# Stick-breaking attention block: the turns of the attention weights of small query tiles, and the turns of v, gathered into fewer bunches on TensorE

## The reference, cut to what matters

```python
for blk in range(seq // Q_BLOCK):                      # Q_BLOCK = 128
    z = einsum('bhqd,bhkd->bhqk', qb, kb) * scale      # keys 0 .. (blk+1)*128
    log_one_minus = where(mask, log_sigmoid(-z), 0)
    suffix = cumsum(log_one_minus, reverse=True) - log_one_minus
    weights = where(mask, exp(log_sigmoid(z) + suffix), 0)
    out = einsum('bhqk,bhkd->bhqd', weights, vb)
```

## Time and profile before

| what | value |
|---|---|
| median of 3 runs | 788.62 us (788.29 to 788.79) |
| profiled execution | 789.4 us, of which the span of instructions is 787.7 us |
| PE busy / loads of weights | 777.6 us (99%) / 662.2 us (84%) |
| DVE busy | 581.3 us (74%) |
| ACT busy | 413.8 us (53%) |
| the four pairs of attention | about 54 to 332 us of the span, 71.0 us each |
| granted TensorE clock | 0.999 |

### The profile page before, as it was taken

One profiled execution on the slowest core, in us unless ns is written; L12 is line 12 of the kernel. 1 busy time (PEld: TensorE's weight loads), 2 busy tenths in 40 slices (PEclk: granted clock), 3 DMA queues, 4 the chain that ended last, 5 costly groups with the idle time before them and its releaser, 6 DMA issues.

```text
span 787.7 us, 11914 instructions
## 1 busy us (share of the span) xinstructions
PE 777.6 (99%) x4458; PEld 662.2 (84%) x4458; DVE 581.3 (74%) x835; ACT 413.8 (53%) x714; POOL 33.0 (4%) x30
## 2 busy tenths in 40 slices
PE   8999999999999999999999999999999999999997
PEld 6888888888888888899899888888888888888886
DVE  6649997988899798832656767755467777779986
ACT  7546666665667476522716554444333333365443
POOL 1560000000000000020000000000000000000000
PEclk9999999999999999999999999999999999999999
DMA  9772121202201121121021001344333333395222
GB/s 319 261 255 54 27 55 53 53 27 53 53 27 33 49 53 32 43 64 54 27 56 27 29 28 54 107 146 140 139 111 107 107 107 107 111 370 214 108 107 107
DMA packets 72484, 76.31 MB, mean 97 GB/s; under 512 B 3805, under 2 KB 57208, under 8 KB 71929
## 3 DMA queue, kind: packets, MB, share of 16 engines
q1 hardware_dynamic: 72242, 75.45, 30.2%
q10 hardware_dynamic: 198, 0.28, 0.1%
HBM read 55.79 MB, written 15.73 MB: 91 GB/s over the span
## 4 chain that ended last, share of the span: by engine, by line
PE 93%; ACT 2%; DVE 2%; issue 1%; DMA 1%; SPq 0%; DVEq 0%; ACTq 0%
PE pj L709 27%; PE pj L834 6%; PE tr L1008 6%; PE sc L957 6%; PE ob L957 6%; PE ob L782 4%; PE ob L1008 4%; PE pj L1008 4%; PE tr L792 4%; PE sc L1008 3%; PE pj L725 3%; PE pj L815 3%; PE sc L758 2%; PE sc L757 2%; PE tr L1064 1%; PE ob L1034 1%
## 5 line engine op out<-in xcount | busy, mean ns | idle before, releaser
L709 PE MATMUL pj<-h_lo,w_hi 128*128 128x512 f32 x336 | 133.2, 396 | 0.0
L709 PE MATMUL pj<-h_hi,w_lo 128*128 128x512 f32 x336 | 132.2, 393 | 0.0
L709 PE MATMUL pj<-h_hi,w_hi 128*128 128x512 f32 x336 | 132.1, 393 | 0.0
L1697 DVE TENSOR_TENSOR_SCAN surv<-surv,diag 128x128 f32<-128x128 f32 (+3 forms) x64 | 86.3, 1349 | 7.4 <-ACT surv L1188 7.1
L709 PEld LDWEIGHTS pj<-h_hi,w_hi 128*128 128x128 f32 x336 | 63.1, 188 | 12.6
L709 PEld LDWEIGHTS pj<-h_hi,w_lo 128*128 128x128 f32 x336 | 63.2, 188 | 12.4 <-issue 0.3
L709 PEld LDWEIGHTS pj<-h_lo,w_hi 128*128 128x128 f32 x336 | 63.1, 188 | 12.4 <-issue 0.2
L1234 ACT ACTIVATE wt_hi<-tr 128x512 fp32r<-128x512 f32 (+2 forms) x96 | 43.6, 490 | 36.5 <-PE tr L792 35.0
L1634 DVE TENSOR_TENSOR w_lo<-w_raw,w_hi 128x1024 fp32r<-128x1024 f32 x33 | 40.3, 1221 | 22.8 <-ACT w_hi L1130 22.6
L1732 DVE TENSOR_TENSOR wt_lo<-tr,wt_hi 128x512 fp32r<-128x512 f32 (+2 forms) x96 | 50.2, 550 | 7.1 <-ACT wt_hi L1234 6.6
L1701 DVE TENSOR_TENSOR beta<-beta,surv 128x128 f32<-128x128 f32 (+3 forms) x64 | 48.6, 759 | 6.5
(11 more groups left out here) (437 smaller groups left out, 1902.9 us busy)
## 6 DMA issues: line engine op xcount, KB each, us to landing
w_raw<-in_w_in SPq DMA_DIRECT2D x30, 512.0 KB, 3.8
y_scratch<-y_ring SPq DMA_DIRECT2D x28, 256.0 KB, 2.1
graw<-in_w_in SPq DMA_DIRECT2D x14, 512.0 KB, 5.1
y_back<-y_scratch SPq DMA_DIRECT2D x14, 512.0 KB, 5.2
x_t<-in_x SPq DMA_DIRECT2D x8, 512.0 KB, 6.7
wrow<-in_w_out SPq DMA_DIRECT2D x4, 1024.0 KB, 9.3
w_scratch<-wsum SPq DMA_DIRECT2D x4, 1024.0 KB, 5.0
wout_raw<-in_w_out SPq DMA_DIRECT2D x8, 512.0 KB, 7.4
```

The costliest lines, as they stand in the source:

```text
L709: mm = pe.matmul(pj[bank][:, :], (w_lo if p == 2 else w_hi)[:, slot, k, :], (h_lo if p == 1 else h_hi)[:, k, HALF * h:HALF * h + HALF], st ...
L1697: dve.tensor_tensor_scan(s[:, ::-1], s[:, ::-1], d[:, ::-1], 0.0, ALU.mult, ALU.add)\
```

## The change

The first unit of each head (1 block) is no longer turned at its own step but together with the second (2 blocks), in one round of three blocks. The third (3 blocks) is turned one step later than before, right in front of the fourth (4 blocks), each in a round of its own. Both rounds of v are turned at step 2, one right behind the other. The rounds of a pair go from 26 to 24. The number of transposes, of copies on ACT and of subtractions on DVE stays. So that the weights of the first and third unit survive one step longer, units 0 and 4 of each head get another place in their slot of `beta` (`beta_at`), and ACT waits for `w_ready` before it writes a slot of `surv` that it had been told by the turn of the unit to be read.

```diff
     for step in range(STEPS):
-        if step in (1, 2):
-            rounds.append(("v", step, step - 1))
-        if 1 <= step <= 16:
-            unit = step - 1
-            blocks = unit % 8 + 1
-            for b in range(0, blocks, 4):
-                rounds.append(("w", step, unit, b, min(4, blocks - b)))
+        if step == 2:
+            rounds += [("v", step, 0), ("v", step, 1)]
+        unit = step - 1
+        if not 1 <= step <= 16 or unit % 8 in (0, 2):
+            continue
+        blocks = unit % 8 + 1
+        if unit % 8 == 1:
+            rounds.append(("w", step, [(unit - 1, 0, 1), (unit, 0, 2)]))
+            continue
+        if unit % 8 == 3:
+            rounds.append(("w", step, [(unit - 1, 0, 3)]))
+        for b in range(0, blocks, 4):
+            rounds.append(("w", step, [(unit, b, min(4, blocks - b))]))
     return rounds
+
+def beta_at(unit):
+    return {0: 7 * P, 4: 3 * P}.get(unit % 8, 0)
...
-LAST_ROUND = {r[2]: n for n, r in enumerate(ROUNDS) if r[0] == "w"}
+LAST_ROUND = {piece[0]: n for n, r in enumerate(ROUNDS) if r[0] == "w" for piece in r[2]}
...
-                            pe.wait_ge(w_ready, 16 * i + unit + 1)
+                            pe.wait_ge(w_ready, 16 * i + r[2][-1][0] + 1)
                             pe.wait_ge(tr_free, RPP * i + R0 + n - 1)
-                            for b in range(nb):
-                                mm = pe.transpose(tr[n % 2][:, P * b:P * b + P],
-                                                  beta[:, unit % 2, P * (b0 + b):P * (b0 + b) + P], ident[:, :])
+                            at = 0
+                            for unit, b0, nb in r[2]:
+                                for b in range(b0, b0 + nb):
+                                    c0 = beta_at(unit) + P * b
+                                    mm = pe.transpose(tr[n % 2][:, at:at + P], beta[:, unit % 2, c0:c0 + P],
+                                                      ident[:, :])
+                                    at += P
                             mm.then_inc(tr_ready, 1)
...
                         act.wait_ge(scores_ready, 16 * i + step + 1)
+                        if step % 8 in (2, 4):
+                            act.wait_ge(w_ready, 16 * i + step - 1)
...
-                        act.activation(beta[:, step % 2, 0:keys].rearrange("p (c w) -> p c w", w=width), scores,
+                        c0 = beta_at(step)
+                        act.activation(beta[:, step % 2, c0:c0 + keys].rearrange("p (c w) -> p c w", w=width), scores,
                                        ACT.Sigmoid, scale=HD ** -0.5).then_inc(sig_done, 1)
-                    if step in (1, 2):
-                        act.wait_ge(wsum_stored[step + 1], 16)
+                    if step == 2:
+                        act.wait_ge(wsum_stored[2], 16)
+                        act.wait_ge(wsum_stored[3], 16)
```

More of the change, by code:

```diff
@@ L787, in pair @@
                         if r[0] == "w" and r[1] == step:
-                            unit, b0, nb = r[2:]
-                            pe.wait_ge(w_ready, 16 * i + unit + 1)
+                            pe.wait_ge(w_ready, 16 * i + r[2][-1][0] + 1)
                             pe.wait_ge(tr_free, RPP * i + R0 + n - 1)
-                            for b in range(nb):
-                                mm = pe.transpose(tr[n % 2][:, P * b:P * b + P],
-                                                  beta[:, unit % 2, P * (b0 + b):P * (b0 + b) + P], ident[:, :])
+                            at = 0
[5 more added lines that the diff above has]
+                                    at += P
                             mm.then_inc(tr_ready, 1)
@@ L1230, in pair @@
                         if r[0] == "w" and r[1] == step:
-                            unit, b0, nb = r[2:]
-                            g = unit % 8 // 2
                             act.wait_ge(tr_ready, RPP * i + R0 + n + 1)
-                            act.activation(wt_hi[g % 2][:, b0:b0 + nb, P * (unit % 2):P * (unit % 2) + P],
-                                           tr[n % 2][:, 0:P * nb].rearrange("p (b q) -> p b q", q=P),
-                                           ACT.Copy).then_inc(tr_act, 1)
+                            at = 0
+                            for unit, b0, nb in r[2]:
+                                g = unit % 8 // 2
+                                cp = act.activation(wt_hi[g % 2][:, b0:b0 + nb, P * (unit % 2):P * (unit % 2) + P],
+                                                    tr[n % 2][:, at:at + P * nb].rearrange("p (b q) -> p b q", q=P),
+                                                    ACT.Copy)
+                                at += P * nb
+                            cp.then_inc(tr_act, 1)
             with act.Fori(0, PAIRS - 1) as i:
@@ L1700, in pair @@
                         dve.wait_ge(sig_done, 16 * i + step + 2)
-                        dve.tensor_tensor(beta[:, step % 2, 0:keys], beta[:, step % 2, 0:keys],
+                        own = beta[:, step % 2, beta_at(step):beta_at(step) + keys]
+                        dve.tensor_tensor(own, own,
                                           surv[:, step % 2, 1:keys + 1], ALU.mult).then_inc(w_ready, 1)
-                    if step in (1, 2):
-                        dve.wait_ge(wsum_stored[step + 1], 16)
+                    if step == 2:
+                        dve.wait_ge(wsum_stored[2], 16)
+                        dve.wait_ge(wsum_stored[3], 16)
                     for n, r in enumerate(ROUNDS):
@@ L1727, in pair @@
                         if r[0] == "w" and r[1] == step:
-                            unit, b0, nb = r[2:]
-                            g = unit % 8 // 2
-                            qs = slice(P * (unit % 2), P * (unit % 2) + P)
                             dve.wait_ge(tr_act, RPP * i + R0 + n + 1)
[L1732 to L1735, removed]
+                            at = 0
+                            for unit, b0, nb in r[2]:
+                                g = unit % 8 // 2
+                                qs = slice(P * (unit % 2), P * (unit % 2) + P)
+                                sub = dve.tensor_tensor(wt_lo[g % 2][:, b0:b0 + nb, qs],
+                                                        tr[n % 2][:, at:at + P * nb].rearrange("p (b q) -> p b q", q=P),
+                                                        wt_hi[g % 2][:, b0:b0 + nb, qs].bitcast(F32), ALU.subtract)
+                                at += P * nb
+                            sub.then_inc(tr_free, 1)
                     if step >= 3 and step % 2:
```

## The result

The changed kernel takes 793.10 us (median of 5, 792.41 to 793.62) against 788.79 us for the kernel before in the same comparison: ratio 1.0053, 95% interval 1.0037 to 1.0069, so 2.9 to 5.4 us slower. One timing of the kernel before, 1110 us, lies 40% above the other four and is left out of the ratio.

What follows compares the result with a forecast made beforehand. PE was taken to bound the kernel; a new 0.92 us stall per pair, less savings at borders and unit 7, added 2.9 us to 788.6, giving 791.5 us. The range was 789.8 to 793.2, the forecast's own 790.6 to 792.4.

Steps and rivals of the forecast that it cites:

- What bounds the kernel: PE, busy 99% of the span, with next to no stall to remove; a new wait adds undiluted.
- the new wait: At step 2 the joint turn of units 0 and 1 waits for DVE's low part of the first v round.
- The size of the stall: Joint turn, step 2: PE ready at 132.69, released at 133.61, so 0.92 us a pair; allowed 0.7 to 1.1.
- the first link: ACT, step 1: without the v copy, `q_st` starts at that copy's old time, 126.93 instead of 127.56.
- The signs named for this place: Steps 1 and 2: `z_sig`, `z_silu`, `w_lo` about 0.6 us earlier; DVE's scan of unit 3 about 0.6 later.
- Borders: Twenty fewer switches between transposes and other matmuls save 0.5 us; bounds 0.01 to 0.09 each, 0.2 to 1.8 in all.
- What is given back: After the stall DVE gains 0.25 us on PE and keeps it until unit 7, removing a wait there.
- unit 7's 0.12 us: PE's wait for DVE at the turn of unit 7, expected to vanish in three of the four pairs.
- One of the signs of being wrong: In the profile after, pairs differing from each other by more than 0.12 us would speak against the forecast.
- The rivals without a stall: Low part of v in time: cheap borders, about 788.1 us, 10 in 100; or borders 0.09 each, 786.4, 4 in 100.
- the one with 1.55 us: Joint turn: DVE's chain starts at its old time, stall 1.55 us a pair, 793.9 us total; 9 in 100.
- the one in which half of it is swallowed: DVE-bound places further on absorb half the stall: about 1.5 us slower, 790.1 us; 7 in 100.

Runs made afterwards that it cites:

- e1: Kernel before with only the v rounds changed: both turned at step 2, every weight turn left in place; 794.41 us, ratio 1.0060.
- e2: Kernel before with only the weights gathered as in the change, v turned at steps 1 and 2 as before; 788.96 us, ratio 0.9991.
- e7: The changed kernel with both v rounds turned together at step 1 instead of step 2; 788.17 us, ratio 0.9998 to the kernel before.
- e3: The changed kernel with DVE's two low parts of v at step 2 moved ahead of the scan of unit 2; 788.62 us, ratio 0.9992 to before.
- e5: The changed kernel with a useless DVE copy of 256 columns ahead of the first low part of v; 794.02 us, ratio 1.0069 to before.
- e6: The changed kernel with the w_lo subtraction moved from the end of step 1 to behind step 2's low parts of v; 787.87 us, ratio 0.9994 to before.
- e4: Kernel before with 28 bunches split by a held-back projection matmul, adding 28 borders; 789.82 us, ratio 1.0003, stretch +0.19 us.

## Why the prediction was right, and where its terms were off

**What bounds the kernel, and the new wait: right.** One new wait a pair, at the joint turn, for the first low part of v, reached by reading the order of banks against DVE's order. e1, e2 and e7 place it in the v rounds at step 2; e3, e5 and e6 show the chain on DVE to be its whole cause.

**The size of the stall: 1.08 us, not 0.92.** PE's request was right: 133.42 - 0.75 = 132.67 against 132.69. The release came at 134.50 - 0.75 = 133.75 against 133.61. The stall is 1.08 - 0.92 = 0.16 longer: 0.02 from the request, and the 0.14 of the release stem from the first link: I let ACT's `q_st` start where the v copy had, 0.27 behind the start of the second sigmoid. It started 0.40 behind it, when the sigmoid had ended, and `z_sig`, `z_silu` and all behind it moved with it. The distances from `z_silu` to the low part of v came out as read (3.29 us forecast and measured). The signs named for this place came, with sizes off in the same way: `z_silu` 0.5 us earlier against the pair's start where 0.6 was expected, DVE's scan of unit 3 0.8 later where 0.6 was. A pair loses 1.11 us by unit 7, 0.03 more than the stall of 1.08. This term the forecast did not have, and it lies right behind the stall: the three transposes and the first score take 0.62 us there (134.50 to 135.12), in e3, without a stall, 0.57 (131.67 to 132.24).

**Borders: 0.5 us forecast, 0 found.** The term "0.04 for the v bunch and 0.02 for each of the other four" was wrong; my lower bound of 0.01 was near the truth (e4: 0.007 at most). The Trainium skill ("TensorE: Matmul & The Clock Gate", section "Single matmul latency") gives a lone matmul about 166 ns that don't depend on its columns; at that price the 28 borders of e4 would have cost an estimated 4.6 us. They cost 0.19. No run here has a lone matmul, so the figure itself is not put to the test; it doesn't apply, because a bunch of transposes doesn't break the stream.

**What is given back: wrong in its mechanism; that the amount came near is luck.** "It goes", of unit 7's 0.12 us, failed: the wait is in every kernel here. DVE did gain on PE (its scan of unit 3 was 1.57 us later than before, 136.21 against 134.64, where PE's score behind the joint turn was 1.84 later, 134.81 against 132.97), but the lead ended at unit 4, where DVE now had to wait for the copy that it had met just in time before (PE's score, kernel before; then the timeline of DVE, kernel before and the change):

```profile
132.97 0.48 PE L757 MATMUL sc<-k_hi,q_st 128*128 128x512 f32 x1
```

```profile
144.74 0.96 DVE L1701 TENSOR_TENSOR beta<-beta,surv 128x768 f32<-128x768 f32 x1
145.74 0.89 DVE L1732 TENSOR_TENSOR wt_lo<-tr,wt_hi 128x512 fp32r<-128x512 f32 x2
```

```profile
146.31 0.96 DVE L1723 TENSOR_TENSOR beta<-beta,surv 128x768 f32<-128x768 f32 x1
147.59 0.69 DVE L1756 TENSOR_TENSOR wt_lo<-tr,wt_hi 128x512 fp32r<-128x512 f32 x1 [0.32 <-ACT wt_hi L1253]
```

From there DVE is exactly as late as PE (147.59 against 145.74, 1.85 us), and unit 7 finds things as they were. That its absence of gaps before meant a full queue was my mistake: a queue without gaps may also be one that is served just in time. In its place came the 0.6 us at the product of step 13 (0.36 had been forecast at unit 7), which the table of waits showed and I had not followed to its cause.

**The sum.** Forecast 4 x 0.92 - 4 x 0.10 - 3 x 0.12 = 2.9. Found 4 x 1.11 - 0.62 = 3.8, against 3.83 us in the stretch. By timings 2.9 to 5.4 us. In the forecast 0.76 us were given back, 0.40 by borders and 0.36 at unit 7, neither of which came; the 0.6 that did is near it by chance.

The forecast's own range, 790.6 to 792.4 or 2.0 to 3.8 us slower, has the stretch's 3.83 just at its end and leaves the median of 793.1 outside. Its lower end was also worked out wrongly: it takes the borders at their value of 0.5, and with the stated bound of 1.8 it would have been about 789.2. One of the signs of being wrong did come, pairs that differ by more than 0.12: at unit 15 the first three had lost 0.93, 0.93 and 0.89 us, the last 1.09, because only the first three have the gain at step 13. The rivals without a stall and the one with 1.55 us are refuted by the stall that all four pairs show, 1.10 to 1.12 us each; the one in which half of it is swallowed, by the 3.83 us that are left at the end of the stretch.

**A version better than both.** The change with DVE's low parts of v first (e3) is clearly faster than the change (0.9992 against 1.0053) and by its timings about 0.1% faster than the kernel before, which its interval (0.9983 to 1.0001) just fails to show.

## What to carry to other kernels

With two buffers in turn, a round waits for the reader of the round two before it; when rounds are regrouped, write down the new order of buffers and look where that reader's instruction now stands in its own engine's queue, with all that is ahead of it. Before merging bunches to save borders, price a border from start times of a bunch of one and a bunch of many; here it was nothing. And a queue that shows no gaps before may be just in time rather than behind: a lead given to it need not last beyond the next hand-over.

## What the runs showed that I had not expected

Going from wide matmuls to transposes and back costs PE at most 0.007 us, although PE's starts look uneven there: the matmul behind a lone transpose starts 0.03 us behind it (145.15 to 145.18 in e4) and the next one 0.28 later. Only the distance over the whole border tells the price. On ACT, two sigmoids and the copy of v overlapped (the copy started 0.27 behind the start of a sigmoid 0.38 long), while `q_st` in the same place began only 0.40 behind it; the runs don't say why.
